# Expert weights in 4 MB transfers with 32 KB runs from the third group of experts on

## What is computed

```python
N_EXPERTS, TOP_K, D_EXPERT = 32, 4, 1024
for e in range(N_EXPERTS):
    gu = t @ w_gate_up[e] + b_gate_up[e]          # (1024, 2048)
    gate = jnp.minimum(gu[:, :D_EXPERT], SWIGLU_LIMIT)
    up = jnp.clip(gu[:, D_EXPERT:], -SWIGLU_LIMIT, SWIGLU_LIMIT)
    h = (up + 1.0) * (gate * jax.nn.sigmoid(SWIGLU_ALPHA * gate))
    out = out + comb[:, e:e + 1] * (h @ w_down[e] + b_down[e])   # (1024, 1024)
```

## Time and profile before

| | |
|---|---|
| median of 3 runs | 1214.67 us |
| the profiled execution | 1214.78 us, of which 1213.1 us from the first to the last instruction |
| TensorE (PE) busy | 1184.2 us, 98% |
| 16 DMA engines, last 3/4 of the span | full, 426 to 431 GB/s |
| moved by SP's queue | 440.30 MB |
| VectorE, ScalarE, GpSimd busy | 27%, 18%, 2% |

### The profile page before, as it was taken

The page is one execution under the profiler, slowest core; times in us unless marked ns, Lnnn a source line. Parts: engine busy times, 40 slices in busy tenths (PEclk is TensorE's granted clock), DMA queues, the critical chain, the costliest instruction groups (busy, mean ns, idle before and its releaser), DMA issues.

```text
span 1213.1 us, 14490 instructions
## 1 busy us (share of the span) xinstructions
PE 1184.2 (98%) x5813; PEld 569.3 (47%) x5813; DVE 322.7 (27%) x812; ACT 214.9 (18%) x421; POOL 29.1 (2%) x64
## 2 busy tenths in 40 slices
PE   9999999999999999999999999999999999799997
PEld 7777777443443434343434433434434343334333
DVE  6644214151313221222303130223132212111223
ACT  2656402221010101011010112120101010101024
POOL 2001000000000000000000021000000000000000
PEclk9999999999999999999999999999999999899999
DMA  9935573579999999999999999999999999999951
GB/s 287 366 133 182 186 277 139 204 287 429 426 425 425 429 425 428 428 426 431 426 431 426 430 426 426 427 429 427 427 427 430 426 431 426 427 427 427 430 237 39
DMA packets 53143, 446.81 MB, mean 368 GB/s; under 512 B 8159, under 2 KB 11455, under 8 KB 28409
## 3 DMA queue, kind: packets, MB, share of 16 engines
q1 hardware_dynamic: 50512, 440.30, 87.6%
q0 software_dynamic: 2464, 5.71, 1.6%
q10 hardware_dynamic: 112, 0.03, 0.0%
HBM read 444.51 MB, written 1.88 MB: 368 GB/s over the span
## 4 chain that ended last, share of the span: by engine, by line
PE 85%; DMA 13%; DVE 1%; issue 1%; ACT 1%; SPq 0%; DVEq 0%
PE ps L1183 32%; PE ps L846 16%; PE ps L1197 15%; DMA ring<-in_w_down 11%; PE ps L1046 8%; PE ps L1211 4%; PE ps L998 2%; PE ps L1318 2%; PE ps L1145 2%; DMA ring<-in_w_in 2%; PE ps L1135 1%; PE ps L880 1%; PE ps L840 1%; PE ps L1235 0%; ACT L1676 0%
## 5 line engine op out<-in xcount | busy, mean ns | idle before, releaser
L1183 PE MATMUL ps<-ring,work 128*64 128x512 f32 x2000 | 440.5, 595 | 0.3 <-DVE work L2018 0.3
L1183 PEld LDWEIGHTS ps<-ring,work 128*64 128x64 f32 x2000 | 140.5, 137 | 269.6 <-issue 261.0
L1197 PE MATMUL ps<-ring,work 128*64 128x512 f32 x992 | 222.6, 594 | 8.1 <-DMA ring<-in_w_down 8.1
L846 PE MATMUL ps<-work,ring 128*128 128x288 f32 x736 | 180.7, 407 | 0.8 <-DMA ring<-in_w_in 0.8
L846 PEld LDWEIGHTS ps<-work,ring 128*128 128x128 f32 x736 | 139.4, 190 | 41.0 <-issue 1.7
L1197 PEld LDWEIGHTS ps<-ring,work 128*64 128x64 f32 x992 | 69.4, 137 | 134.6 <-issue 121.6
L2085 DVE TENSOR_SCALAR work<-ps 128x512 f32<-128x512 f32 x32 | 22.1, 692 | 369.7 <-PE ps L1183 369.7
L1606 ACT ACTIVATE work<-work 128x512 f32<-128x512 f32 x32 | 20.2, 632 | 457.1 <-DVE work L2085 457.1
L2057 DVE TENSOR_TENSOR work<-ps,gain_pairs 128x512 f32<-128x512 f32 x30 | 20.8, 692 | 301.6 <-PE ps L1046 301.6
L1046 PEld LDWEIGHTS ps<-work,x_tok 128*128 128x128 f32 x768 | 91.9, 196 | 13.9 <-issue 13.0
L1046 PE MATMUL ps<-work,x_tok 128*128 128x128 f32 x768 | 95.4, 284 | 0.4 <-DVE work L1966 0.4
(11 more groups left out here) (275 smaller groups left out, 637.7 us busy)
## 6 DMA issues: line engine op xcount, KB each, us to landing
ring<-in_w_gate_up SPq DMA_DIRECT2D x125, 2048.0 KB, 26.3
ring<-in_w_down SPq DMA_DIRECT2D x62, 2048.0 KB, 25.5
ring<-in_w_in SPq DMA_DIRECT2D x7, 2048.0 KB, 18.4
work<-in_w_gate_up SPq DMA_DIRECT2D x3, 1536.0 KB, 11.5
ring<-in_w_proj_b SPq DMA_DIRECT2D x2, 2048.0 KB, 9.0
ring<-in_w_proj_a SPq DMA_DIRECT2D x2, 2048.0 KB, 10.5
ring<-in_w_out SPq DMA_DIRECT2D x2, 2048.0 KB, 9.9
ring<-in_w_ple_gate SPq DMA_DIRECT2D x4, 1024.0 KB, 27.4
```

The lines of the kernel that those rows point to most:

```text
L846: mm = pe.matmul(out(b), lhs, rhs, start=(k == 0), stop=(k == len(pairs) - 1))
L1183: mm = pe.matmul(ps[half(g), b, :], xg[:, k, i % 2, :], blocks[2 * (k % 2) + at][:, 512 * g:512 * g + 512], start=False, stop=(k == KC - 1))
L1197: mm = pe.matmul(ps[half(g), b, :], hT_of[i % 2][:, 4 * j + k, :], blocks[k][:, 512 * g:512 * g + 512], start=False, stop=(4 * j + k == KC ...
```

## The change

From group 2 on, two pieces that follow each other (both of one half of `w_gate_up`, or both of `w_down`) come in one transfer of 4 MB into two neighbouring places of the ring. A partition now gets 32 KB that lie together in HBM: 4 rows of `w_gate_up` or 8 of `w_down` (`RUN` = 4). Groups 0 and 1 keep 2 MB transfers, each of one half (16 KB) of such a run. The very last two pieces are issued apart, the last with its own semaphore. The places of the ring are renumbered (`FRONT`, `MOE_SLOT`, `spare`) so that pairs are neighbours; it is the same schedule under other numbers.

To match the new rows, the gather takes every fourth channel; the gate and up products take their output columns, and the biases with them, dealt in turn to the two halves in runs of four (`dealt`); the transposes of the hidden rows stay as they were.

```diff
-FRONT = [("in", 0, 0), ("in", 2, 1), ("in", 4, 2), ("in", 1, 3), ("in", 3, 4), ("in", 5, 5),
-         ("in", 6, 0), ("in", 7, 1), ("b", 0, 2), ("b", 1, 3), ("a", 0, 4), ("a", 1, 5),
-         ("out", 0, 0), ("out", 1, 1)]
-MOE_SLOT = [6, 7, 2, 3, 4, 5, 0, 1]
+FRONT = [("in", 0, 7), ("in", 2, 0), ("in", 4, 3), ("in", 1, 4), ("in", 3, 5), ("in", 5, 6),
+         ("in", 6, 7), ("in", 7, 0), ("b", 0, 3), ("b", 1, 4), ("a", 0, 5), ("a", 1, 6),
+         ("out", 0, 7), ("out", 1, 0)]
+
+MOE_SLOT = [1, 2, 3, 4, 5, 6, 7, 0]
+RUN = 4
...
-        spare = ring[:, 6:8, :, :].rearrange("p s a b -> p (s a b)")
+        spare = ring[:, 1:3, :, :].rearrange("p s a b -> p (s a b)")
...
+        last_landed = sem("last_landed")
...
+        def two_pieces(q):
+
+            return ring[:, MOE_SLOT[q]:MOE_SLOT[q] + 2, :, :].rearrange("p s a b -> p (s a b)")
+
+        def dealt(row, g):
+
+            return row.rearrange("p (c g k) -> p c g k", g=2, k=RUN)[:, :, g, :]
...
+        def landed_for(Q, i, q):
+
+            at = STREAM.index((i, q))
+            if not (isinstance(Q, int) and Q < OPENING):
+                at = at // 2 * 2
+            return piece_landed[place(Q, *STREAM[at])[0]]
...
-            eng.wait_ge(piece_landed[s], turn * 16 + 16)
+            if not (isinstance(Q, int) and Q < OPENING):
+                _, turn = place(Q, *STREAM[STREAM.index((i, q)) // 2 * 2])
+            eng.wait_ge(landed_for(Q, i, q), turn * 16 + 16)
...
-            def expert_piece(r, q, e):
+            def expert_rows(q, e):
 
                 if q < GU_PIECES:
-                    src = gu_rows[bass.ds(e * D + 2 * P * q, 2 * P), :].rearrange("(p k) c -> p (k c)", k=2)
-                else:
-                    src = dn_rows[bass.ds(e * D + 4 * P * (q - GU_PIECES), 4 * P), :] \
-                        .rearrange("(p k) c -> p (k c)", k=4)
-                sp.dma_start(whole_piece(r), src).then_inc(piece_landed[r], 16)
-
-            def quad_pieces(quads, e0):
-
-                for at in range(QUAD_PIECES):
-                    ring_place_used(quads, at)
+                    return gu_rows[bass.ds(e * D + RUN * P * (q // 2), RUN * P), :] \
+                        .rearrange("(p k) c -> p (k c)", k=RUN)
+                return dn_rows[bass.ds(e * D, D), :].rearrange("(p k) c -> p (k c)", k=2 * RUN)
+
+            def expert_piece(r, q, e, signal):
+
+                sp.dma_start(whole_piece(r), expert_rows(q, e)[:, RUN * D * (q % 2):RUN * D * (q % 2) + RUN * D]) \
+                    .then_inc(signal, 16)
+
+            def quad_pieces(quads, e0, last=False):
+
+                for at in range(0, QUAD_PIECES, 2):
                     i, q = STREAM[at]
-                    expert_piece((at - EXTRAS) % SLOTS, q, e0 + i)
+                    r = (at - EXTRAS) % SLOTS
+                    if last and at == QUAD_PIECES - 2:
+                        ring_place_used(quads, at)
+                        expert_piece(r, q, e0 + i, piece_landed[r])
+                        ring_place_used(quads, at + 1)
+                        expert_piece((r + 1) % SLOTS, q + 1, e0 + i, last_landed)
+                        continue
+                    ring_place_used(quads, at + 1)
+                    sp.dma_start(two_pieces(r), expert_rows(q, e0 + i)).then_inc(piece_landed[r], 16)
 
             def piece_rows(n):
 
                 quads, at = divmod(n, QUAD_PIECES)
                 i, q = STREAM[at]
-                e = 4 * quads + i
-                if q < GU_PIECES:
-                    return w_gate_up[0, e, 2 * P * q:2 * P * q + 2 * P, :].rearrange("(p k) c -> p (k c)", k=2)
-                rows = 4 * P * (q - GU_PIECES)
-                return w_down[0, e, rows:rows + 4 * P, :].rearrange("(p k) c -> p (k c)", k=4)
+                return expert_rows(q, 4 * quads + i)[:, RUN * D * (q % 2):RUN * D * (q % 2) + RUN * D]
...
-            quad_pieces(more * QUADS + (QUADS - 2), LAST)
+            quad_pieces(more * QUADS + (QUADS - 2), LAST, last=True)
...
-            pool.dma_start(gain_pairs[:].rearrange("p (j k) -> p j k", k=2),
-                           g_moe[0].rearrange("(j p k) -> p j k", p=P, k=2)).then_inc(gain_landed, 16)
+            pool.dma_start(gain_pairs[:].rearrange("p (j k) -> p j k", k=RUN),
+                           g_moe[0].rearrange("(j p k) -> p j k", p=P, k=RUN)).then_inc(gain_landed, 16)
...
-            x_blocks = [x_tok[:, t, :].rearrange("p (j c k) -> p j k c", c=P, k=2) for t in range(TT)]
-                return pe.matmul(ps[:, b, (c % 4) * P:(c % 4) * P + P], x_blocks[t][:, c // 2, c % 2, :], sel[t],
+                return pe.matmul(ps[:, b, (c % 4) * P:(c % 4) * P + P], x_blocks[t][:, c // RUN, c % RUN, :], sel[t],
...
+                    row = bias_parts[0:BIAS_ROWS, at:at + D]
                     pe.matmul(ps[half(g), b, :], pick[0:BIAS_ROWS, :],
-                              bias_parts[0:BIAS_ROWS, at + 512 * g:at + 512 * g + 512],
+                              row[:, 512 * g:512 * g + 512] if kind == "out" else dealt(row, g),
...
-                                           blocks[2 * (k % 2) + at][:, 512 * g:512 * g + 512],
+                                           dealt(blocks[2 * (k % 2) + at], g),
...
-            def weigh_down(Q, i, j):
-                blocks = wait_expert_piece(pe, Q, i, GU_PIECES + j)
+                if ends:
+                    pe.wait_ge(last_landed, 16)
+                    rows = whole_piece(place(Q, i, GU_PIECES + j)[0])
+                    blocks = [rows[:, D * k:D * k + D] for k in range(4)]
+                else:
+                    blocks = wait_expert_piece(pe, Q, i, GU_PIECES + j)
...
-                    weigh_down(Q, i + 1, 1)
+                    weigh_down(Q, i + 1, 1, ends=last and j == 1)
```

More of the change, by code:

```diff
@@ L705, in opening_piece @@
                 i, q = STREAM[at]
-                expert_piece(ring_turn(n) % SLOTS, q, 4 * later + i)
+                r = ring_turn(n) % SLOTS
+                expert_piece(r, q, 4 * later + i, piece_landed[r])
             wait_filled(sp, ("gate", 3, 3))
@@ L719, in _ @@
                 i, q = STREAM[at]
-                expert_piece(at, q, i)
+                expert_piece(at, q, i, piece_landed[at])
             extra_rest()
@@ L1040, in _ @@
             turn_residual(1, 0)
-            x_blocks = [x_tok[:, t, :].rearrange("p (j c k) -> p j k c", c=P, k=2) for t in range(TT)]
+            x_blocks = [x_tok[:, t, :].rearrange("p (j c k) -> p j k c", c=P, k=RUN) for t in range(TT)]
             def gather_block(b, c, t, start, stop):
-                return pe.matmul(ps[:, b, (c % 4) * P:(c % 4) * P + P], x_blocks[t][:, c // 2, c % 2, :], sel[t],
+                return pe.matmul(ps[:, b, (c % 4) * P:(c % 4) * P + P], x_blocks[t][:, c // RUN, c % RUN, :], sel[t],
                                  start=start, stop=stop)
@@ L1189, in weigh_gate_up, with weigh_down @@
                         mm.then_inc(piece_used_up[q], 1)
-            def weigh_down(Q, i, j):
+            def weigh_down(Q, i, j, ends=False):
                 b = CHUNK["out", i % 2][0]
-                blocks = wait_expert_piece(pe, Q, i, GU_PIECES + j)
+                if ends:
[4 more added lines that the diff above has]
+                    blocks = wait_expert_piece(pe, Q, i, GU_PIECES + j)
                 for k in range(4):
```

## The result

The changed kernel takes 1289.67 us (median of 4 runs, 1289.27 to 1292.66) against 1214.58 us before, a ratio of 1.0615, 95% interval 1.0601 to 1.0629. It is 75 us slower. The forecast was 1213.2 us, with a range up to 1221.

A forecast was written before the change was run, and what follows sets the result against it. DMA was taken as the bound, by 4 us a pair over TensorE. With 5.6 us of DMA time gained and 4 taken back by lump and gather, -1.6 us turned 1214.78 into 1213.2 us; range 1208.5 to 1221.

The forecast's parts named there:

- What bounds the kernel: Whole kernel: DMA is the bound, 59.1 us a pair against TensorE's 55.05; TensorE's waits for weights total 10.0 us.
- third rival: Slower gather loads make TensorE the bound from 0.78 us a gather on; up to +43 us, 1258; chance 0.12.
- Term 3, the gather: Gather's loads at 16 B spacing: 10 ns more each, 0.48 us a gather, 7.7 us for 16 gathers.
- the rule's case: Gather falls from two hits in a 16 B line to one, and becomes the bound; chance 0.12, slower.
- The gather becomes the bound: Same as the third rival: slower gather loads put TensorE over DMA, up to +43 us, 1258; chance 0.12.
- Term 1, the pace: Weight transfers of groups 2 to 7: 32 KB packets 0.8% faster, last landing 5.6 us earlier.
- second rival: Weight transfers: the pace does not rise with 32 KB runs, the lump remains; +3.1 us, 1217.9; chance 0.17, slower.
- Term 2, the lump: TensorE's waits for down weights: both halves land together, +3.45 us at D1, +2.1 us in the last pair.
- For pair 13 the sum: Chain from pair 13's wait to the end: -4.7 + 3.45 - 1.8 us, plus 2 gathers of 0.48: -2.1 us.
- What costs nothing: Dealt output columns, hidden-row transposes, SP's transfers and renumbered places: put at 0; the DMA engines don't run dry.
- The dealt columns: Output columns read in runs of 16 B, the bias in runs of 8 B: put at no cost.

The follow-up runs named there:

- e10_hidden_4B: The kernel before with the transposes of the hidden rows (L1135) read contiguously instead of 16 B apart: 1214.60 us.
- e7_before_gather_12B: The kernel before with the gather's elements 12 B apart (every third channel): 1245.99 us, a single execution.
- e1_gather_8B: The changed kernel with only the gather's spacing taken back to 8 B (every second channel): 1229.86 us, ratio 1.0118 against the kernel before.
- e3_4MB_16KB_runs: The kernel before with 4 MB transfers from group 2 on, still 16 KB runs, old rows and old gather: 1216.30 us, ratio 1.0014.
- e6_beats_both: e5_stores_apart with old rows and gather in groups 0 and 1, tokens rewritten in pair 3 for contiguous gathers afterwards: 1212.34 us, ratio 0.9979 against the kernel before.
- e5_stores_apart: e1_gather_8B with the output states in other memory, so the embedding's copies no longer wait for their stores: 1212.30 us, ratio 0.9977 against the kernel before.

## Why the prediction was wrong

- **What bounds the kernel: right.** 10 us of slack on TensorE's side decided everything, and the 0.78 us for a gather beyond which TensorE is the bound (third rival) was passed sevenfold.
- **Term 3, the gather: the step that failed.** It put 10 ns on a load and at most 69, from L1135 against L1235, "a contiguous transpose loads faster than other matmuls do, so it has more to lose". Measured: 134 ns (196 to 330), 5.55 us a gather in place of 0.48. Even the upper end, 3.3 us a gather and 1258 us, was short, and the range stopped at about 1 us a gather. The row was read rightly (e10_hidden_4B), the step from it to another kind of load was not: the argument why it must be an upper end was mine, and no row showed it. A price taken over from another form is no bound. That the two kinds already differ when contiguous, 140 and 189 ns for 128 columns, should have warned me that they need not pay the same. The rule of two hits in a line on the SBUF — State Buffer page of the Trainium skill (door 1), which I named against the change, holds here: 8 B apart, two hits, costs 4 ns over contiguous, and 16 B, one hit, costs 137. The same note calls a stride of "4 fp32" free; taken as 16 B from element to element, that is not so here, and the measurement decides. I gave the rule's case 0.12.
- **The rival's time.** "The gather becomes the bound" had the mechanism, the sum -10.0 + 16 x (what a gather adds) and the end at +43; with 5.55 us it gives +78.8, measured +75.1. At 12 B apart (8.63 us a gather) it gives +33.4, measured +31 (e7_before_gather_12B).
- **Term 1, the pace: right.** 0.8% forecast, 428 to 431 GB/s measured (e1_gather_8B), and the second rival falls. In the changed kernel itself it can't be seen, as the engines are not full there.
- **Term 2, the lump: right in kind.** +1.7 us (0.6 to 2.8) for 2.6 forecast in e3_4MB_16KB_runs. For pair 13 the sum said 4.7 us earlier and 3.45 later; in e6_beats_both the second half of D1 starts at 1037.90 + 3.45 = 1041.35 for 1042.53, 1.2 us earlier for 1.25.
- **Missing: who shares the engines with the long packets.** "What costs nothing" looked at TensorE and SP alone and not at GpSimd's stores. In the changed kernel this costs nothing, as the gather hides it, but without the gather it is 17.6 us (e1_gather_8B against e5_stores_apart). A forecast with a free gather would have been off by that.
- **The dealt columns: right in the main.** L1209's 16 records stay at 3.60 us; the bias, put at 0, rises from 0.62 to 0.64 us, in all by 0.8 us of TensorE's time (20.5 to 21.3).

## To carry to other kernels

When a DMA layout is made coarser, follow the new row order to whoever must match it: here a weight load that went from two elements in a 16 B line to one cost some 74 us against 2.6 gained, and one rewrite of the operand into contiguous order (9.4 us of an idle engine), with the stores moved off the path, took it all back. Longer packets are a little faster and make every small transfer on another queue of the same engines wait longer, so look for a wait on such transfers before lengthening them. Where both TensorE and DMA look full, work out each one's period; the difference, 4 us in 59 here, is what any new cost may use up.

## What the runs showed of the hardware

- A 128 x 128 fp32 weight load of the gather takes 192 ns at 4 B between elements, 196 at 8, 261 at 12, 329 at 16 and 335 at 32: beyond 64 lines of 16 B each line more costs 2.1 ns, or each line with a single element 1.0 ns. In a transpose the step from 4 to 16 B costs 69 ns, half as much.
- 16 engines move 385 GB/s with packets of 2 KB (one window of 10 us), 428 with 16 KB and 431 with 32 KB. An estimate from these: a fixed part of about 10 ns in each packet. Fewer transfers of the same packets change nothing (428).
- 640 small packets on GpSimd's queue beside a full SP queue took 29.4 us with 16 KB packets on the other queue (30.7 with 4 MB transfers of such packets) and 51 us with 32 KB. The DMA: Bandwidth & Descriptors page of the Trainium skill (section on queues, rings and completion order) says that an engine goes round its queues packet by packet; both times agree with that, at 40 small packets for each engine.
- A moving fp32 operand of 512 columns in runs of 16 B, every second such run skipped, goes at the pace of a contiguous one (595 ns a record either way). With bf16, in runs of 8 B, the mean record of L1171 takes 409 ns for 399.
